# First weights and first tile of two stages placed in shared on-chip space ahead of the stage

## What is computed

```python
proj = x @ w_in          # 1024 x 2464: rq, rk, rv, rg (512 each), cq 256, ckv 128, kr 32
# forward scan over 128-token chunks (rq, rk, rv), backward scan from the last chunk to the first
o = fwd + bwd
ret_out = silu(rg) * group_norm(o)
q = rms_norm(cq) @ mla_w_uq;  kv = rms_norm(ckv) @ mla_w_ukv
mla_out = rms_norm(attention(q_nope, q_rope, k_nope, k_rope, v))      # 8 heads
x = layer_norm(alpha * x + concat(ret_out, mla_out) @ w_out)
```

## Time and profile before

| | |
|---|---|
| runs | 3655.18, 3649.64, 3655.11 us; median 3655.11 |
| profiled execution: its time | 3652.21 us |
| profiled execution: its span | 3650.4 us |
| busy PE / PEld / DVE / ACT / POOL | 3440.6 / 2936.9 / 2216.9 / 1571.4 / 831.6 us |
| mean granted TensorE clock | 0.972 of full speed |
| stage 1 to 2 | last instruction of stage 1 ends at 490.5, first product of stage 2 at 502.32 us |
| stage 3 to 4 | last instruction of stage 3 ends at 1727.8, first product of stage 4 at 1744.82 us |
| transfers | 506.10 MB, mean 139 GB/s |

### The profile page before, as it was taken

How to read it: one execution, slowest core, us unless ns; L and a number is a source line. 1 busy time by engine, 2 the same in 40 slices (tenths; PEclk the granted TensorE clock), 3 DMA queues, 4 the chain that set the end, 5 groups by cost and what they waited for, 6 DMA issues and landing times. The chain is left out here.

```text
span 3650.4 us, 51341 instructions
## 1 busy us (share of the span) xinstructions
PE 3440.6 (94%) x18881; PEld 2936.9 (80%) x18882; DVE 2216.9 (61%) x3905; ACT 1571.4 (43%) x2018; POOL 831.6 (23%) x412
## 2 busy tenths in 40 slices
PE   7999979997999999998899769999999999999996
PEld 6888868885777777776677559999999999999996
DVE  5444457676888888886555465555555555555578
ACT  2111134444767677676323313333333333333466
POOL 0000000005667677676111101111111111111101
PEclk9999989997999999999899879999999999999998
DMA  4333357766213333110433325555555555555676
GB/s 147 108 109 109 109 195 247 264 242 163 42 32 57 58 57 57 33 32 13 169 135 135 121 84 168 167 167 167 167 167 167 167 167 167 167 167 167 191 255 211
DMA packets 348112, 506.10 MB, mean 139 GB/s; under 512 B 106288, under 2 KB 242224, under 8 KB 342736
## 3 DMA queue, kind: packets, MB, share of 16 engines
q1 hardware_dynamic: 335104, 458.56, 39.7%
q0 software_dynamic: 12880, 45.88, 5.6%
HBM read 366.02 MB, written 138.36 MB: 138 GB/s over the span
## 5 line engine op out<-in xcount | busy, mean ns | idle before, releaser
L63 PE MATMUL psum<-xeT_hi,w_hi 128*128 128x320 f32 x2048 | 634.6, 310 | 0.0
L65 PE MATMUL psum<-xeT_hi,w_lo 128*128 128x320 f32 x2048 | 633.0, 309 | 0.0
L64 PE MATMUL psum<-xeT_lo,w_hi 128*128 128x320 f32 x2048 | 633.0, 309 | 0.0
L1339 POOL TENSOR_TENSOR added<-added,p_hi 128x1024 f32<-128x1024 f32 x192 | 459.0, 2391 | 158.0 <-ACT p_hi L1293 157.1
L2249 DVE TENSOR_TENSOR w_lo<-w_raw,w_hi 128x2048 fp32r<-128x2048 f32 x190 | 427.5, 2284 | 32.3 <-ACT w_hi L2084 32.3
L2084 ACT ACTIVATE w_hi<-w_raw 128x2048 fp32r<-128x2048 f32 x192 | 358.5, 1908 | 188.5 <-PE psum L65 187.2
L1375 DVE TENSOR_TENSOR p_lo<-psum,p_hi 128x1024 fp32r<-128x1024 f32 x272 | 332.3, 1222 | 90.0 <-ACT psum L1295 88.5
L63 PEld LDWEIGHTS psum<-xeT_hi,w_hi 128*128 128x128 f32 x2048 | 384.5, 188 | 0.9
L64 PEld LDWEIGHTS psum<-xeT_lo,w_hi 128*128 128x128 f32 x2048 | 384.5, 188 | 0.6
L65 PEld LDWEIGHTS psum<-xeT_hi,w_lo 128*128 128x128 f32 x2048 | 384.5, 188 | 0.0
L1293 ACT ACTIVATE p_hi<-psum 128x1024 fp32r<-128x1024 f32 x272 | 279.1, 1026 | 219.7 <-PE psum L65 219.7
(11 more groups left out here) (358 smaller groups left out, 7068.6 us busy)
## 6 DMA issues: line engine op xcount, KB each, us to landing
w_raw<-in_w_gate SPq DMA_DIRECT2D x64, 1024.0 KB, 6.1
w_raw<-in_w_up SPq DMA_DIRECT2D x64, 1024.0 KB, 7.6
w_raw<-in_w_down SPq DMA_DIRECT2D x64, 1024.0 KB, 5.4
xT<-xaT SPq DMA_DIRECT2D x20, 1024.0 KB, 6.4
rec<-rec SPq DMA_DIRECT2D x20, 768.0 KB, 3.6
recb<-rec SPq DMA_DIRECT2D x20, 768.0 KB, 5.4
xa<-in_x SPq DMA_DIRECT2D x20, 512.0 KB, 4.9
cq_hi<-xT SPq DMA_DIRECT2D x20, 512.0 KB, 6.3
```

The costliest lines, as they stand in the source:

```text
L63: pe.matmul(out, a[0], b[0], start=first, stop=False)
L64: pe.matmul(out, a[0], b[1], start=False, stop=False)
L65: return pe.matmul(out, a[1], b[0], start=False, stop=last)
L1339: g.tensor_tensor(acc[:], so_far, p_hi[at % 4][:].bitcast(F32), ALU.add).then_inc(s["p_added"], 1)
```

## The change

One tensor, shared (128 x 9224 float32), and the xT buffer of odd tiles, xT_last, are now allocated for the whole program. Each stage uses shared for buffers that it allocated itself before.

- Stage 1: the weight staging, x, the rotary table and one scratch tile lie in shared. Before the transfers for tile 18, SP issues the first 6 raw pieces of wb into shared, where w_in's staging has been used up; at the stage's end SP waits for them too. The last tile's xT (tile 19 is odd) stays in xT_last; it is still stored.
- Stage 2: pieces 0 to 5 need no load and no wait; PE reads x of u = 0 from xT_last. rec, gate, states and scratch lie in shared. SP's list begins with rec of u = 0, then pieces 6 and 7, the table of u = 0, x of u = 1.
- Stage 3: four of the eight p buffers and the two sum buffers lie in the latents that stage 2 has used up. SP issues the 8 pieces of w_out (512 KB each) at slots 22 and 24 of heads 1 to 4, counted from 0, and at slot 20 of the last head feature_w, ret of tile 0 and, behind a wait until o of the blocks so far has been stored, o of tile 0. At the stage's end SP waits for all eleven.
- Stage 4: no load of w_out, feature_w or cat of tile 0. For tile 0 the transposes, the weighing and the splitting are done in halves of 512 columns, so that the first half needs no scaling; the transposes of tile 1 stand behind piece 4 and its squares, root and scaling ahead of piece 4's split; DVE's wait for the constants moves into tile 1's layer norm.
- Stage 5: the raw buffers, one hi buffer (in xT_last) and y_part lie in the kept space.

```diff
+def wo_raw(c, k):
+
+    return c.shared[:, D * k:D * (k + 1)]
+
+
+WB = RW + LAT
+WB_AHEAD = 6
+
+
+def wb_raw(c, k):
+
+    return c.shared[:, WB * k:WB * (k + 1)]
+
+
+def first_cat(c):
+
+    return c.shared[:, DK * D:DK * D + D]
+
+
+def feature_weights(c):
+
+    return c.shared[:, 9 * D:9 * D + DK]
+
...
+    c.shared = ctx.enter_context(nc.sbuf_tensor("shared", [P, 9 * D + DK], F32))
+    c.xT_last = ctx.enter_context(nc.sbuf_tensor("xT_last", [P, 2, DK, P], F32R))
...
-    stage = [ph.enter_context(c.nc.sbuf_tensor(f"{name}_stage{b}", [P, width], F32)) for b in range(n_stage)]
+    stage = [c.shared[:, width * b:width * (b + 1)] for b in range(n_stage)]
...
-        x = [sb(f"xa{b}", [P, D]) for b in range(2)]
-        xT = [sb(f"xaT{b}", [P, 2, DK, P], F32R) for b in range(2)]
+        x = [c.shared[:, (6 + b) * D:(7 + b) * D] for b in range(2)]
+        xT = [sb("xaT0", [P, 2, DK, P], F32R), c.xT_last]
+        ahead_in = c.sem("a_ahead_in")
         x_hi, x_lo = ([t[:, a, :, :] for t in xT] for a in range(2))
-        rt = [sb(f"rope{b}", [P, 2, P]) for b in range(2)]
+        rt = [c.shared[:, 8 * D + 2 * P * b:8 * D + 2 * P * (b + 1)].rearrange("p (a n) -> p a n", a=2) for b in range(2)]
...
+                    if isinstance(t, int) and t == NT - 2:
+                        sp.wait_ge(w_ready, DK)
+                        w_rows = d["w_in"][:, W:W + WB].rearrange("(k p) n -> k p n", p=P)
+                        for k in range(WB_AHEAD):
+                            sp.dma_start(wb_raw(c, k), w_rows[k]).then_inc(ahead_in, 16)
...
+                sp.wait_ge(ahead_in, 16 * WB_AHEAD)
...
-        rec = [sb(f"recb{b}", [P, 3, RH, RD]) for b in range(2)]
-        gate = [sb(f"gate{b}", [P, RW]) for b in range(2)]
-        state = [sb(f"stateb{b}", [P, RH, RD]) for b in range(2)]
-        decayed, weighted, o = sb("decayedb", [P, RH, RD]), sb("weightedb", [P, RH, RD]), sb("ob", [P, RH, RD])
+        BEHIND = WB_AHEAD * W
+        rec = [records(BEHIND), records(0)]
+        gate = [shared(RW * b, RW) for b in (3, 4)]
+        state = [wide(BEHIND + RW * b) for b in (3, 4)]
+        decayed, weighted, o = (wide(RW * b) for b in (5, 6, 7))
...
-        raw = [krT[:, 0:W], krT[:, W:2 * W], raw_more[0][:], raw_more[1][:],
-               rec[1][:].rearrange("p a h e -> p (a h e)")[:, 0:W], raw_more[2][:]]
+        raw = [wb_raw(c, k) for k in range(WB_AHEAD)] + [krT[:, 0:W], krT[:, W:2 * W]]
         raw_of, raw_before, raw_arrivals = [], [], []
         for k in range(NRAW):
-            buf = k if k < 6 else k - 6 if k < DK else k % 3
+            buf = k if k < DK else (WB_AHEAD, WB_AHEAD + 1, WB_AHEAD - 1)[k % 3]
             raw_before.append(max((m + 1 for m in range(k) if raw_of[m] == buf), default=0))
             raw_of.append(buf)
-            raw_arrivals.append(16 * raw_of.count(buf))
+            raw_arrivals.append(16 * (raw_of.count(buf) - (buf < WB_AHEAD)))
...
-                load_raw(0)
+                load_rec(0)
+                for k in range(WB_AHEAD, DK):
+                    load_raw(k)
                 load_x(0)
-                for k in range(1, DK):
-                    load_raw(k)
-                load_rec(0)
                 load_x(1)
                 sp.wait_ge(s["w_lo_made"], 6)
                 sp.dma_start(lw[:], d["latent_w"]).then_inc(s["lw_in"], 16)
...
                 def project_first():
-                    pe.wait_ge(x_in[0], 32)
                     for k in range(DK):
                         pe.wait_ge(s["w_lo_made"], k + 1)
-                        x_k, first, last = (x_hi[0][:, k, :], x_lo[0][:, k, :]), k == 0, k == DK - 1
+                        x_k, first, last = (c.xT_last[:, 0, k, :], c.xT_last[:, 1, k, :]), k == 0, k == DK - 1
...
-                        pe.wait_ge(x_in[b], 32 * (u // 2 + 1))
+                        wait_from_one(pe, x_in[b], 32 * ((u + 1) // 2))
...
                 def split_hi(k):
-                    a.wait_ge(raw_in[raw_of[k]], raw_arrivals[k])
+                    wait_from_one(a, raw_in[raw_of[k]], raw_arrivals[k])
...
-        added = [sb(f"added{b}", [P, 2, 512]) for b in range(2)]
+        wide = lambda at: at.rearrange("p (z n) -> p z n", z=2)
+        added = [wide(latents[4][:, D * b:D * (b + 1)]) for b in range(2)]
...
-        p_hi = [sb(f"p_hi{b}", [P, 2, 512], F32R) for b in range(4)]
-        p_lo = [sb(f"p_lo{b}", [P, 2, 512], F32R) for b in range(4)]
+        p_hi, p_lo = ([wide(latents[2 + a][:, D * b:D * (b + 1)]) for b in range(2)]
+                      + [sb(f"p_{n}{b}", [P, 2, 512], F32R)[:] for b in (2, 3)] for a, n in enumerate(("hi", "lo")))
...
+        AHEAD_LOADS = {SLOTS * (n // 2 + 1) + 22 + 2 * (n % 2): n for n in range(DK)}
+        FIRST_CAT = SLOTS * (MH - 1) + 20
...
+                    if g in AHEAD_LOADS:
+                        k = AHEAD_LOADS[g]
+                        sp.dma_start(wo_raw(c, k), d["w_out"][k * P:(k + 1) * P, :]).then_inc(ahead_in, 16)
+                    if g == FIRST_CAT:
+                        sp.dma_start(feature_weights(c), d["feature_w"]).then_inc(ahead_in, 16)
+                        sp.dma_start(first_cat(c)[:, 0:RW], d["ret"][0]).then_inc(ahead_in, 16)
+                        for b in range(2):
+                            sp.wait_ge(o_out[b], 16 * sum(1 for n in range(NBH) if n % 2 == b and turn_at[n] + 1 <= g))
+                        sp.dma_start(first_cat(c)[:, RW:D], d["o"][0].rearrange("p h e -> p (h e)")
+                                     ).then_inc(ahead_in, 16)
                     if g >= SLOTS and j == 3 and h < MH - 1:
...
+                sp.wait_ge(ahead_in, 16 * (DK + 3))
...
-        load_w, w_make_hi, w_make_lo, w_ready = split_weights(c, ph, "wo", d["w_out"], w_hi, w_lo, D, 6)
...
-                load_cat(0, 0)
-                sp.dma_start(fw[:], d["feature_w"]).then_inc(s["fw_in"], 16)
-                load_w(sp)
...
+                def turn_first():
+                    for half, done in ((0, "turned_a"), (1, "turned")):
+                        if half == 1:
+                            pe.wait_ge(s["scaled"], 1)
+                        for k in range(4):
+                            at = 4 * half + k
+                            ins = pe.transpose(ps[:, half, k * P:(k + 1) * P], cat[0][:, at * P:(at + 1) * P], c.ident)
+                        ins.then_inc(s[done], 1)
+
...
                 def project_first():
-                    pe.wait_ge(s["lo_made"], 1)
+                    pe.wait_ge(s["lo_a_made"], 1)
                     for k in range(DK):
-                        pe.wait_ge(w_ready, k + 1)
+                        if k == 4:
+                            pe.wait_ge(s["lo_made"], 1)
+                        pe.wait_ge(s["w_lo_made"], k + 1)
                         for half in range(2):
                             cols = slice(half * 512, (half + 1) * 512)
                             ins = mm3(pe, ps[:, 2 + half, :], (cat_hi[0][:, k, :], cat_lo[0][:, k, :]),
                                       (w_hi[:, k, cols], w_lo[:, k, cols]), k == 0, k == DK - 1)
                             if k == DK - 1:
                                 ins.then_inc(s[f"half{half}"], 1)
-                    turn(1, 1)
+                        if k == 4:
+                            turn(1, 1)
 
...
-                turn(0, 0)
+                turn_first()
...
-                        scale(u + 1, 1 - b, u * 16 + (32 if b == 0 else 48))
+                    if there(u, 1) and not is_first(u):
+                        scale(u + 1, 1 - b, u * 16 + (32 if b == 0 else 16))
                     if there(u, -1):
...
-                scale(0, 0, 32)
-                make_hi(0, 0)
-                w_make_hi(a)
+                def w_make_hi(k):
+                    a.activation(w_hi[:, k, :], wo_raw(c, k), ACT.Copy).then_inc(s["w_hi_made"], 1)
+                scale(0, 0, 0)
+                a.wait_ge(s["weighted_a"], 1)
+                a.activation(cat_hi[0][:, 0:4, :], weighted[:, 0:4, :], ACT.Copy).then_inc(s["hi_a_made"], 1)
+                w_make_hi(0)
+                a.wait_ge(s["weighted"], 1)
+                a.activation(cat_hi[0][:, 4:DK, :], weighted[:, 4:DK, :], ACT.Copy).then_inc(s["hi_made"], 1)
+                for k in range(1, DK):
+                    if k == 4:
+                        scale(1, 1, 32)
+                    w_make_hi(k)
                 per_tile(a, slot)
...
+                        if isinstance(u, int) and u == 1:
+                            v.wait_ge(s["const_in"], 48)
...
                         weigh(u + 1, 1 - b)
-                v.wait_ge(s["fw_in"], 16)
+                def weigh_first(half, turned, weighted_done, hi_done, lo_done):
+                    ks = slice(4 * half, 4 * half + 4)
+                    v.wait_ge(turned, 1)
+                    v.tensor_tensor(weighted[:, ks, :], ps[:, half, :].rearrange("p (k n) -> p k n", k=4),
```

(19 more changed lines are left out.)

71 lines of the change are left out of this document (39 added, 32 removed).

## The result

Four runs of the changed kernel took 3628.35 to 3631.88 us, median 3629.75; four of the kernel before, taken together with them, 3649.64 to 3655.18, median 3653.44. The ratio is 0.9935, 95% interval [0.9919, 0.9951]. The profiled execution took 3629.22 us with a span of 3627.4, 23.0 less than before.

What follows compares the result with a forecast made beforehand. PE was taken as the bound, so moved loads gain only where it stands still, at the starts of stages 2 and 4. 7.2 + 10.3 = 17.5 us off the mean 3653.0 gave 3635.5 us, range 3630 to 3644.

Steps and rivals of the forecast that it cites:

- Stage 4, I take 10.3, within 7.5 and 11: Start of stage 4: tile 1 begins earlier; gain taken as 10.3 us, 7.5 if the clock rises 3.5 us later.
- The moved p and sum buffers have the same shapes: nothing: Stage 3: moving these buffers was forecast to cost nothing, since their shapes stay the same.
- Stage 2, gain 7.2: Start of stage 2: first product's end at 509.4 against 516.63, gain 7.2 us; 5.4 if the clock rises after 7.1.
- Stage 3, "nothing": Stage 3: the early transfers of 512 KB, the moved buffers and the wait for o were each costed at nothing.
- stage 3 longer than 892 us: Sign of being wrong: attention, stage 3, takes more than 892 us.
- four signs of being wrong: ACT waiting for krT at piece 6; clock 0.50 beyond 5 us; DVE's resid waiting for PE; stage 3 over 892 us.
- ACT's wait for krT at piece 6: Sign of being wrong, in stage 2: ACT has to wait for krT at piece 6.
- a clock of 0.50 beyond 5 us: Sign of being wrong: granted clock 0.50 beyond 5 us in either first product, stage 2 or stage 4.
- A: Rival: clock stays low through both first products of stages 2 and 4; gain 2.9 us, 3650, no change; chance 0.03.
- B: Rival: engines not ready when stages 2 and 4 begin; 7.2 us lost, 3642.7, still faster; chance 0.06.
- C: Rival: early w_out pieces hold up rows of maxima in stage 3; 33.6 us lost, 3669, slower; chance 0.03.

Runs made afterwards that it cites:

- late_wo: The changed kernel with w_out's eight pieces loaded at the start of stage 4 again and none during attention; median 3635.71 us (3632.17 to 3637.13).

## Why the prediction was right and wrong

**Direction, and the mechanism of the two starts: right.** Both starts went as written. PE's first products came 2.2 and 6.1 us after SP's first issue where 2.4 and 6.3 were forecast, tile 1's product 23.4 where 24 was. Undoing single parts puts 5.9 (pieces), 3.4 (first tile) and 1.7 us (order) on the parts, 11.0 of stage 4's 11.2 until tile 1's product.

**The step that failed: "Stage 4, I take 10.3, within 7.5 and 11".** The term was measured at 17.0, and its upper end was the wrong one. 11.2 are the start, 0.9 more than taken. 1.7 are tile 1's period, most of it the high clock (0.23 of it is the pace): the forecast priced the clock inside the first product alone, though the earlier trace rows show tile 1's product at 0.77 us behind a wait of 4.88, which the change shortens. 4.1 are the pace, and here it was the sentence "The moved p and sum buffers have the same shapes: nothing" that failed, said of stage 3 and silently held for every stage: in stage 4 buffers moved that nobody meant to move, and with them the distance between the two operands; of all that moved, only feature_w's 32 bytes change what the distance leaves by 512. Nothing in the trace of before showed that such a thing has a price; only runs could. Without the pace's 4.1 and the 0.2 in tile 1's period the median would be at some 3634 us by this account, inside the range.

**"Stage 2, gain 7.2" was nearly right, by two errors.** The product's end moved 6.6 us, since the clock stayed low for 5.3 us and not 3.6, inside the bound of 7.1. 2.4 us more came from short falls of the clock which before had behind it and the changed kernel did not. These differ from profile to profile: stage 2 takes 331.9 to 335.8 us in the eight with the change's stage 2 (mean 333.2) and 338.8 to 342.2 in the ten with before's (mean 341.0). By the means the gain is 7.8, and the rest of 9.0 is chance.

**Stage 3, "nothing".** Right for the eight loads and the moved buffers. The 3.7 us are the clock's fall at attention's end, earlier in one execution than in another; "stage 3 longer than 892 us" was also no useful mark, since before had 895.4 itself by the reading used here.

**Signs.** Of the four signs of being wrong three appeared: ACT's wait for krT at piece 6 (0.77 us), a clock of 0.50 beyond 5 us (5.3 and 6.1) and the length of stage 3. None of them is what took the time out of the range; the quicker pace of the products, which did, had no sign there.

**Rivals.** A (clock low through both products) did not happen: it stood at 0.50 for 5.3 and 6.1 us in the two. B (engines not ready): ACT began 0.01 us after SP in both stages. By the rule of the Trainium skill that stood behind B (Runtime: NRT & Kernel Launch, Instruction fetch mechanics) the branch could have cost more; whatever it costs lies within the 3.5 to 4.9 us from a stage's last instruction to the next one's first, which both kernels have (3.5 and 4.5 before, 3.5 and 4.9 after). C (late rows of maxima): the one such wait is 3.6 us after the change against 4.2.

**The range** took the spread of the times and the ends of the terms, and had no room for a term that was missing. Its lower end was short by 0.25 us; the chances, 0.93 for faster, stood.

## What to carry to other kernels

Where PE is the bound, compare the distance between moving and stationary operand in a partition before and after any change to the allocation: in two stages of this kernel a multiple of 512 bytes (256 in the one kernel that tried it) made each 512-column float32r product 2% quicker than the other distances tried, worth 4.1 and some 8 us of the profiles, for a few hundred unused bytes. When a stage starts late, look for what is queued behind the transfer, not only at what it feeds: in late_wo w_out delayed the first product by 0.2 us, and tile 1's cat behind it held up tile 1's by 5.9. (No run put that cat ahead of w_out.) And a last stretch with idle PE pays for its clock: fourteen products that nobody reads took attention to 895.3 us in both kernels that had them, from a mean of 898.5.

## What the runs showed of the hardware

The pace of products depends on where the two operands lie relative to each other: 24 products of 512 columns take 5.30 to 5.34 us in the mean, or 5.43 to 5.45, from the first's start to the last's, at the same granted clock of 1.00. Shifting both by 32 bytes changes nothing. Distances that leave 32, 64 or 128 when divided by 512, and in stage 1 288, were the slow ones; those that leave 0, and the one that leaves 256, the quick ones. The Trainium skill (TensorE: Matmul & The Clock Gate, Part 2: What happens when you issue a matmul) gives TensorE two independent read ports, one for each operand, and a pace of one column a cycle. By that one would not expect the distance to matter; the measurements say that it does. Why it matters was not found, and whether 256 bytes suffice in stage 1, or in stage 2, whose weight rows are 3712 bytes long so that the distance changes with every k, wasn't tried.

From a stage's first product to the clock's rise it took 5.3 us in stage 2 and 6.1 in stage 4 after the change, 7.3 and 3.8 before (the rows end at 7.1 and 3.8). It fell during the last, thinly filled 13 us of attention in 17 of the 18 profiles without extra products there; between before and after, with the same 40 instructions on PE, that moved attention by 3.7 us.
